# A decoder layer in one kernel: finer waits in the mixer, the merge and the two paired weight blocks

## The reference

```python
xn = rmsnorm(x, g_norm_mix)
proj = xn @ w_in                                  # conv b/c/h, q/k/v, z, a, beta, two merge gates
y_a = (b_c * causal_conv(c_c * h_c)) @ w_out_a    # branch a
o   = gated_delta_chunked(q, k, v, g, beta, s0)
y_b = (normed(o) * silu(z)) @ w_out_dn            # branch b
gate_a, gate_b = jnp.split(jax.nn.sigmoid(gates), 2, axis=-1)
h = x + (gate_a * y_a + gate_b * y_b) @ w_o
h = h + peer(rmsnorm(h, g_norm_ffn), w_query, ...)   # 8 heads, 16 of 16384 experts per token
return rmsnorm(h, g_norm_final)
```

## Time and profile before

| | us |
|---|---|
| median of 3 runs | 3488.58 |
| lowest, highest | 3487.09, 3494.86 |
| span of the profiled execution, first to last instruction | 3500.7 |
| PE busy in it | 3350.9 (96%) |
| DVE busy | 2591.7 (74%) |
| ACT busy | 1018.7 (29%) |
| POOL busy | 977.2 (28%) |

### The profile page before, as it was taken

How to read it: one execution, slowest core, us unless ns; L and a number is a source line. 1 busy time by engine, 2 the same in 40 slices (tenths; PEclk the granted TensorE clock), 3 DMA queues, 4 the chain that set the end, 5 groups by cost and what they waited for, 6 DMA issues and landing times.

```text
span 3500.7 us, 56614 instructions
## 1 busy us (share of the span) xinstructions
PE 3350.9 (96%) x21384; PEld 3291.5 (94%) x21384; DVE 2591.7 (74%) x4995; ACT 1018.7 (29%) x1349; POOL 977.2 (28%) x773
## 2 busy tenths in 40 slices
PE   6999999999998999998998899999999999999996
PEld 6999999899998999998997899999999999999996
DVE  5554444233343379999997899999999999999996
ACT  5742222321322232222543122222222222222222
POOL 0000000000000111111002555555555555555550
PEclk8999999999999999999999999999999999999998
DMA  2111011111322232334889999899998999999992
GB/s 105 40 45 36 29 36 64 68 48 42 141 85 73 89 107 102 106 112 136 266 266 307 333 337 328 318 327 326 338 329 317 327 327 340 328 321 321 329 326 104
DMA packets 304353, 698.46 MB, mean 200 GB/s; under 512 B 23873, under 2 KB 124225, under 8 KB 303201
## 3 DMA queue, kind: packets, MB, share of 16 engines
q0 software_dynamic: 98592, 362.97, 28.5%
q1 hardware_dynamic: 104112, 276.89, 23.3%
q10 hardware_dynamic: 101520, 56.89, 5.3%
HBM read 604.44 MB, written 92.22 MB: 199 GB/s over the span
## 4 chain that ended last, share of the span: by engine, by line
PE 77%; DVE 17%; DMA 2%; DVEq 2%; ACT 1%; issue 1%; ACTq 0%; SPq 0%; PEldq 0%
PE PS L1532 29%; PE PS L365 16%; PE PS L1515 14%; PE PS L1223 6%; PE PS L1253 5%; DVE HOTG L2052 3%; PE PS L1447 3%; PE PS L380 1%; DVE HOT L2048 1%; DVE HOT L2049 1%; DVE fold L1980 1%; DVE besti L1924 1%; DVE sc L1915 1%; DVE besti L1916 1%; DVEq L1978 1%
## 5 line engine op out<-in xcount | busy, mean ns | idle before, releaser
L1532 PE MATMUL PS<-AH,VH 128*128 128x368 f32 x2048 | 513.8, 332 | 20.4 <-DVE VL L2075 10.9
L1532 PE MATMUL PS<-AH,VL 128*128 128x368 f32 x2048 | 515.2, 332 | 0.0
L1532 PE MATMUL PS<-AL,VH 128*128 128x368 f32 x2048 | 509.7, 330 | 0.0
L746 POOL DMA_INDIRECT SLOT<-rows_u,EID x256 | 346.4, 1353 | 578.5 <-DVE XLF L2091 257.5
L746 POOL DMA_INDIRECT SLOT<-rows_v,EID x256 | 333.7, 1304 | 205.7 <-DVE SLOT L2082 167.5
L1532 PEld LDWEIGHTS PS<-AH,VH 128*128 128x128 f32 x2048 | 365.2, 189 | 22.7 <-DVE VL L2075 12.1
L1532 PEld LDWEIGHTS PS<-AL,VH 128*128 128x128 f32 x2048 | 366.2, 189 | 0.0
L1532 PEld LDWEIGHTS PS<-AH,VL 128*128 128x128 f32 x2048 | 365.8, 189 | 0.0
L2091 DVE SCALAR_TENSOR_TENSOR XLF<-SLOT,GA,XLF 128x1024 f32<-128x1024 f32 x256 | 328.0, 1281 | 0.5 <-DMA SLOT<-rows_v,EID 0.2
L1109 ACT ACTIVATE VH<-VRAW 128x512 fp32r<-128x512 f32 x256 | 157.8, 628 | 567.7 <-PE PS L1532 567.7
L2082 DVE SCALAR_TENSOR_TENSOR SLOT<-SLOT,XHF 128x1024 f32<-128x1024 f32 x256 | 312.6, 1221 | 3.3 <-DMA SLOT<-rows_u,EID 3.3
(11 more groups left out here) (331 smaller groups left out, 6478.3 us busy)
## 6 DMA issues: line engine op xcount, KB each, us to landing
RAW<-experts_u SPq DMA_DIRECT2D x128, 512.0 KB, 6.4
VRAW<-experts_v SPq DMA_DIRECT2D x256, 256.0 KB, 5.8
gate_matrices<-stg ACTq DMA_DIRECT2D x21, 2048.0 KB, 10.2
GW<-gate_matrices SPq DMA_DIRECT2D x96, 384.0 KB, 7.2
RAW<-weights SPq DMA_DIRECT2D x69, 512.0 KB, 3.6
activations<-AS SPq DMA_DIRECT2D x64, 368.0 KB, 2.4
AS<-activations SPq DMA_DIRECT2D x64, 368.0 KB, 3.0
GW<-gate_matrices SPq DMA_DIRECT2D x32, 320.0 KB, 6.0
```

The source lines that it names most:

```text
L746: pool.indirect_dma_start(out=SLOT[n % NSLOT][:, :], out_offset=None, in_=table, in_offset=bass.IndirectOffsetOnAxis(ap=ids, axis=0)).then ...
L1532: mm = pe.matmul(PS[:, 4 + 2 * (d % 2) + t, 0:CH], w[:, d % 2, c * P:c * P + P], x[:, c, t * CH:t * CH + CH], start=(c == 0 and n == 0), s ...
```

## The change

It has three parts. (1) `pair_products` takes the two blocks together for the first five chunks only, then the last three chunks of the first block and after them the last three of the second. (2) Ahead of the Y loop PE no longer waits for `bl_done` but for `free_c` (set 1 read), and the BH unit waits chunk by chunk; `free_c` 18 (set 0 read) stands ahead of the OH unit. The two initial counts of `y_read` and of `free_h` are given early. (3) XH and XL of a merged row are made within the Y loop, right after the row's add, by ACT and DVE; the W_o units wait for set 1 and set 0 to be read (`y_read` 17 and 18) and chunk by chunk for `ml_done`, which they did before. 

```diff
--- before.py
+++ after.py
@@ -371,16 +371,19 @@
 
         def pair_products(pe, first, base):
 
-            for k in range(KD):
-                pe.wait_ge(xl_done, base + k + 1)
-                for s in (first, 1 - first):
-                    for n in range(3):
-                        for t in range(3):
-                            w, x = ((WH, XH), (WH, XL), (WL, XH))[n]
-                            mm = pe.matmul(PS[:, 3 * s + t, 0:TH], w[:, s, k * P:k * P + P],
-                                           x[:, k, t * TH:t * TH + TH], start=(k == 0 and n == 0), stop=(k == KD - 1 and n == 2))
-                    if k == KD - 1:
-                        mm.then_inc(unit_done, 1)
+            both = KD - 3
+            order = [(k, s) for k in range(both) for s in (first, 1 - first)]
+            order += [(k, s) for s in (first, 1 - first) for k in range(both, KD)]
+            for k, s in order:
+                if s == first:
+                    pe.wait_ge(xl_done, base + k + 1)
+                for n in range(3):
+                    for t in range(3):
+                        w, x = ((WH, XH), (WH, XL), (WL, XH))[n]
+                        mm = pe.matmul(PS[:, 3 * s + t, 0:TH], w[:, s, k * P:k * P + P],
+                                       x[:, k, t * TH:t * TH + TH], start=(k == 0 and n == 0), stop=(k == KD - 1 and n == 2))
+                if k == KD - 1:
+                    mm.then_inc(unit_done, 1)
 
         rms_sems = {n: {k: sem(f"{n}_{k}") for k in ("sq", "sum", "mm", "ln", "rn")} for n in ("na", "nb", "nc")}
 
@@ -988,11 +991,8 @@
                     row = HID[:, ds(2 * i + q, 1), :].rearrange("p n t -> p (n t)")
                     act.activation(row, row, ACT.Sigmoid).then_inc(sig_done, 1)
                     act.activation(sig[:, q, :], sig[:, q, :], ACT.Sigmoid).then_inc(sig_done, 1)
-
-            act.wait_ge(m_done, KD)
-            act.wait_ge(unit_done, filled(unit_of(B_O - 1)))
-            for k in range(KD):
-                act.activation(XH[:, k, :], HID[:, k, :], ACT.Copy).then_inc(mh_done, 1)
+                    act.wait_ge(m_done, 2 * i + (q + 1))
+                    act.activation(XH[:, ds(2 * i + q, 1), :].rearrange("p n t -> p (n t)"), row, ACT.Copy).then_inc(mh_done, 1)
 
             with act.Fori(0, KD // 2) as i:
                 for r in range(2):
@@ -1383,19 +1383,24 @@
                     products(pe, 1 - r, 1 - r, XH, XL).then_inc(unit_done, 1)
 
             pe.wait_ge(ol_done, H)
-            pe.wait_ge(bl_done, H)
+            pe.wait_ge(free_c, B_Y - B_Z + 1)
             with pe.Fori(0, KD // 2) as i:
                 for q in range(2):
                     pe.wait_ge(lo_done, 2 * i + (B_Y + q + 1))
                     pe.wait_ge(y_read, 4 * i + (2 * q + 1))
-                    products(pe, (1 + q) % 2, 1, BH, BL, range(0, H)).then_inc(unit_done, 1)
+                    products(pe, (1 + q) % 2, 1, BH, BL, range(0, H), ready=(bl_done, 0) if q == 0 else None).then_inc(unit_done, 1)
+                    if q == 0:
+                        pe.wait_ge(free_c, B_Y - B_Z + 2)
                     pe.wait_ge(y_read, 4 * i + (2 * q + 2))
                     products(pe, (1 + q) % 2, 0, OH, OL, range(H, KD), H).then_inc(unit_done, 1)
 
+            pe.wait_ge(y_read, 2 * KD + 1)
             with pe.Fori(0, KD // 2) as i:
                 for r in range(2):
                     pe.wait_ge(lo_done, 2 * i + (B_O + r + 1))
                     pe.wait_ge(free_h, 2 * i + (r + 1))
+                    if r == 1:
+                        pe.wait_ge(y_read, 2 * KD + 2)
                     products(pe, 1 - r, 1 - r, XH, XL, ready=(ml_done, 0) if r == 0 else None).then_inc(unit_done, 1)
             pe.wait_ge(free_h, KD + 2)
             rms_pe(pe, rms_sems["nb"], rn)
@@ -1787,6 +1792,8 @@
                     g_lows(NPAIR, f"d{s}")
             dve.wait_ge(l2_ln, 2 * H + 1 + H)
             dve.drain().then_inc(free_c, 2)
+            dve.drain().then_inc(y_read, 2)
+            dve.drain().then_inc(free_h, 2)
             g_lows(NPAIR, "s")
             for h in range(H):
                 row = QKV[:, h, :]
@@ -1848,7 +1855,6 @@
                 dve.wait_ge(bh_done, i + 1)
                 dve.tensor_tensor(BL[:, i, :], bc[:, :], BH[:, i, :].bitcast(F32), ALU.subtract).then_inc(bl_done, 1)
 
-            dve.drain().then_inc(y_read, 2)
             with dve.Fori(0, KD // 2) as i:
                 for q in range(2):
                     row = thirds(HID[:, ds(2 * i + q, 1), :].rearrange("p n t -> p (n t)"))
@@ -1861,10 +1867,10 @@
                     dve.tensor_tensor(thirds(sig[:, q, :]), pset(0), thirds(sig[:, q, :]), ALU.mult).then_inc(y_read, 1)
                     dve.drain()
                     dve.tensor_tensor(row, row, thirds(sig[:, q, :]), ALU.add).then_inc(m_done, 1)
-            dve.drain().then_inc(free_h, 2)
-            for k in range(KD):
-                dve.wait_ge(mh_done, k + 1)
-                dve.tensor_tensor(XL[:, k, :], HID[:, k, :], XH[:, k, :].bitcast(F32), ALU.subtract).then_inc(ml_done, 1)
+                    dve.wait_ge(mh_done, 2 * i + (q + 1))
+                    dve.tensor_tensor(thirds(XL[:, ds(2 * i + q, 1), :].rearrange("p n t -> p (n t)")), row,
+                                      thirds(XH[:, ds(2 * i + q, 1), :].rearrange("p n t -> p (n t)")).bitcast(F32),
+                                      ALU.subtract).then_inc(ml_done, 1)
 
             rms_zero(dve, rms_sems["nb"], rn)
             with dve.Fori(0, KD // 2) as i:
```

## The result

| | before | changed |
|---|---|---|
| median, us | 3491.72 (4 runs) | 3475.89 (4 runs) |
| lowest, highest | 3487.09, 3495.04 | 3472.35, 3479.23 |
| span of the profiled execution | 3500.7 | 3474.6 |

The ratio is 0.9947, with a 95% interval of 0.9935 to 0.9959: 18.5 us of 3491.7 gained, between 14.3 and 22.7. Forecast were 3468.8 us and a gain of 19.8, within 3463 to 3477.

What follows compares the result with a forecast made beforehand. PE, busy 96% of the span, was taken as the bound, so its waits cost time. Gains of 5.7 + 2.3 + 4.4 + 7.4 = 19.8 us from 3488.6 gave 3468.8 us, range 3463 to 3477.

Steps and rivals of the forecast that it cites:

- Bound: Whole kernel: PE busy 96% of the span, so its waits are kernel time; four single waits make 15.9 us.
- First pair: Unit behind the first pair: gap 4.25 to 1.35 us, full clock behind it; 2.9 + 2.8 = 5.7 us gained.
- rival (b): Unit behind the first pair still starts slow: 17.0 us won, 3471.6 us; chance 0.10.
- Second pair: Behind the second pair: WL no longer late, 2.3 us gained; rows already fast, so no clock to win.
- Entry of the Y loop: First Y units start early, the third waits 2.6 us for the gates' product; 4.4 us gained, not 6.9.
- rival (a): New gap of 2.6 us at the third Y unit takes the clock down: 17.6 us won, 3471.0 us; chance 0.16.
- (a) and (b) together: Clock falls at the third Y unit and the unit behind the first pair starts slow: 3473.8 us; chance 0.04.
- Split in the loop: First W_o unit starts 5.5 us earlier and loses 1.9 us of slow rows: 7.4 us, with 1.4 us to spare.
- Rival (c): Y loop: table loads cost ACT twice their length, two-load halves 1.2 us late, four times; 3473.4 us, chance 0.04.
- Rival (d): Loop entries: another wait still holds PE, parts 2 and 3 give nothing; 8.0 us won, 3480.6 us, chance 0.06.
- Rival (e): Y loop: ring of ACT and DVE turns slower than PE; at 15.5 us 41.6 lost, 3510 us; chance 0.03.
- Behind 1118 us: Everything later hangs on PE or chains starting from it and moves as a block; clock falls worth 2 us either way.

Runs made afterwards that it cites:

- six copies: Changed kernel with six more ACT copies to XH in each Y-loop turn, each with a drain: 3505.49 us, 1.0033 of the kernel before.
- three copies: Changed kernel with three more ACT copies to XH in each Y-loop turn, each with a drain: 3486.22 us, 0.9978 of the kernel before.

## Why the prediction came out as it did

**Bound.** Right for the four entries: in each trace the stretch around an entry that is gone is shorter by it, or by what the next wait leaves of it. It doesn't hold of the whole list: the waits for WL in the expert part (L1447 before), which no part touches, come to 7.7 to 14.6 us over the ten profiles, and the times don't follow them.

**First pair, 5.7 us.** The gap went as written, 1.34 us left for 1.35. The slow rows went too: with the pairs the unit behind is 11.8 us long in all seven profiles that have them, so rival (b) didn't happen. What the forecast had too large is what stood there before. It took 14.56 us from the one profile at hand; the two other kernels without the pairs have 13.17 and 13.95:

```profile
59.57 1.22 PE L365 MATMUL PS<-XH,WH 128*128 128x352 f32 x3 [4.25 <-ACTq L785]
...
72.74 0.38 PE L1199 MATMUL PS<-C,ab 4*128 4x4 f32 x2
```

This is the kernel with the BH and BL waits alone. The same gap of 4.25 us cost 1.3 to 2.7 us of slow rows, and the term is 4.3 to 5.7, not 5.7.

**Second pair, 2.3 us.** With the pairs alone the stretch from the first W_o read to the first row behind the query units is 194.3 us, before 196.7, and with either of the other parts alone 196.7 as well: 2.4. The idle time was right. In the changed kernel WL is there at 1095.73 and PE comes at 1096.46:

```profile
1094.50 1.23 DVE L352 TENSOR_TENSOR WL<-RAW,WH 128x1024 fp32r<-128x1024 f32 x1 [6.51 <-ACT WH L347]
...
1096.46 0.65 PE L365 MATMUL PS<-XH,WH 128*128 128x352 f32 x3
```

But "no clock to win" held in one profile only. Three kernels have this gap of 2.13 us: in before the rows behind it are fast, in the kernels with the waits alone and with the split alone they are slow. The latter:

```profile
1104.38 1.18 PE L365 MATMUL PS<-XH,WH 128*128 128x352 f32 x3 [2.13 <-DVE WL L352]
1105.36 1.08 PE L365 MATMUL PS<-XL,WH 128*128 128x352 f32 x3
```

In the two profiles of the changed kernel the stretch is 3.0 and 3.2 us shorter than before; slow rows at other places of it differ too, so the term is 2.4 to 3.2.

**Entry of the Y loop, 4.4 us.** The step that mattered held: a finer wait gives what the next wait leaves, here the gates. Forecast was a gap of 2.6 us; it is 2.19, since the gates land 0.2 us sooner behind the BL and PE follows DVE after 0.05 us, not 0.15. Then rival (a) came true: the clock fell at this gap in both profiles of the changed kernel and in that of the waits alone (2.19, 2.15, 2.11 us). The two kernels with extra copies have the gap too (2.26, 2.19 us), and there it stayed up. The window's granted clock shows it (columns as in the earlier trace rows):

```profile
880.00:885.00 5.00, 4.74 (x20) 4.74 (x21) 3.57 (x4) 2.16 (x3) 0.94 (x2) 0.66 0.10 14
```

0.66, where 1.00 is 2.4 GHz and 0.50 is 1.2. With it the place is worth 4.6 - 1.7 = 2.9 us in this trace and 2.4 in the kernel with this part alone; rival (a) priced it at 4.4 - 2.2 = 2.2. Its 2.2 us of slow rows came without a working of their own, between the 1.9 and 2.9 taken from other places; the three falls cost 1.65 to 1.67, under both. The term that failed is the 4.4, and what failed in it was the chance of 0.16 (0.20 with the case of (a) and (b) together) for a fall behind a gap this long, where three of five profiles show one. The Trainium skill, "TensorE: Matmul & The Clock Gate", section "Loop structure matters more than you think", says that a long wait for a transfer between every two matmuls makes PE go cold. The waits here are short, 2.1 to 2.3 us, and the clock fell at three of five all the same; with the transfers taken out of the way it stayed up.

**Split in the loop, 7.4 us.** Right in every piece: 74.58 - 69.12 = 5.5 us and 13.88 - 11.95 = 1.9, against 5.5 and 1.9. The middle says 7.6 with this part alone. The runs say 5.9, with an interval that holds 7.4. The cover has 1.25 us left for 1.4 forecast.

**Rival (c)**, table loads at twice their length, would have made gaps in every second turn; none is there, and the activation starts 0.02 us behind its load (876.43 + 1.28, then 877.73). The drain of 1.38 us that the Trainium skill gives beside each load in "ScalarE: Activation LUTs", section "What ACT_TABLE_LOAD costs", isn't seen in this loop, neither ahead of a load (896.46 + 1.08 = 897.54, then 897.56) nor behind one. **Rival (d)** is refuted by the entry that is gone, in the kernel with that part alone.

**Rival (e)'s price** was too high: 41.6 us for a ring of 15.5, counted as 4.0 of waiting and 1.2 of slow rows in each of eight turns. With six copies the turns are (16.8 + 14.3) / 2 = 15.6 us and the loss 29.0. It is paid in seven turns, not eight, since the first row's product stands ahead of all copies. And where the ring sets the pace a turn lasts as long as the ring, and slow rows lie inside PE's next wait: the turns from 911.23 and from 942.37 both last 14.3 us, the first at full pace with 2.54 us of wait at its end, the second with slow rows and 0.96. Only where PE is the bound again, as with three copies, do slow rows add.

**The sum and the level.** By the traces the terms are 4.3 to 5.7, 2.4 to 3.2, 2.4 to 2.9 and 7.4 to 7.6: 16.5 to 19.4 us in place of 19.8, and the runs say 18.5. That is 1.3 us of the 7.1. Another 2.7 are the distance between the ratio's 18.5 and the 15.8 by which the two medians of four runs differ, and 3.1 are the level: the forecast put the gain under the median of the first three runs, 3488.58; with one run more it was 3491.72. Over 29 and 17 runs on two chips it was 3494.87 and 3495.63. The changed kernel repeats within 0.6 us (3475.89, 3476.52). With a level 3 to 7 us too low the time still came within the range, by 1.1 us; that is in part luck. The 12.1 us between span and median of before, which the forecast took as given, seem to be no property of the profiler: in the later kernels each run's own time is 1.7 us above its span (3476.33 and 3474.6). By that rule the profiled execution of before took some 3502.4 us, longer than any other run of it on record (at most 3502.18). The difference of the two spans, 26.1 us, would have told 7.6 too much. Where it comes from is seen in code that the change doesn't touch. Granted clock of 500 to 600 us, before, changed, and changed once more (columns as in the earlier trace rows, the clock is the third number from the end):

```profile
500.00:600.00 100.00, 96.91 (x696) 94.85 (x695) 44.13 (x84) 23.37 (x50) 0.00 (x0) 0.93 0.10 33
```

```profile
500.00:600.00 100.00, 95.73 (x730) 93.35 (x729) 47.37 (x96) 23.38 (x50) 1.07 (x2) 1.00 0.14 44
```

```profile
500.00:600.00 100.00, 97.32 (x702) 95.23 (x701) 42.42 (x79) 23.38 (x50) 1.07 (x2) 0.93 0.11 38
```

One program has 1.00 here once and 0.93 the next time, and gets 730 or 702 matmuls done in the 100 us. Between the first row sums of the q/k/v stage (some 80 us in, L1191 before) and the start of the middle, which no part touches, before took 790.0 us and the nine others 783.1 to 788.5. **Behind 1118 us** the forecast took everything to move as a block. The code from the query units to the last norm took 2285.5 us before and 2281.1 and 2280.9 in the two profiles of the changed kernel, but 2279.1 to 2283.9 in the three kernels with one part each; before is the longest of the ten profiles, but the change can't be told from that spread.

## What to carry to other kernels

A wait made finer is worth the distance to the next thing that is late, so look up when every other input of the unit arrives before counting the old gap as won: here it was two gates' transfers, issued behind an event the change didn't move, and fetching them early was worth 4.1 us more by the trace, where the finer wait itself had given 2.4 to 2.9. Work moved into a loop was free here while its ring of engines was shorter than the turn of PE, the bound; count the ring by its rows, with the handovers, and load it on purpose once to see where it breaks (1.25 us by the trace, 3.4 us put in, 2.1 us late). Take the gain from the gaps, and the level from many runs: the median of three was 6 to 7 us off, and two profiles of different luck differ by more than most edits are worth.

## What the hardware showed that I hadn't expected

**The length of a gap doesn't decide whether the clock falls**, among the gaps seen here of 2.1 to 3.5 us. With three copies, 2.10 us took it down at 905.67 and at 932.63 and not at 959.61, in one loop, with the same rows before and behind; with six copies it fell behind 2.57, 2.54 and 3.44 and not behind 3.46. Behind the second pair's gap of 2.13 us it stayed up in before and fell in two other kernels; in before it stayed up behind 3.19 too. At one and the same place, the third Y unit, it fell behind 2.19, 2.15 and 2.11 us and not behind 2.26 and 2.19. What does decide isn't settled by these runs. The gap of 1.34 us behind the first pair never took it down, in six profiles.

**The clock was low around small matmuls too.** PE is without an idle moment in the transposes of a and beta (4 x 4 tiles, 3.9 to 4.9 us of them, from 68.13 in the changed kernel), and yet within them or behind them the clock is at 0.50 in all ten profiles, for a time that differs between two executions of one program. No run takes the transposes away, so that they are the cause is not shown. Changed, and changed once more:

```profile
72.00:74.00 2.00, 2.00 (x10) 1.98 (x9) 1.84 (x3) 0.00 (x0) 0.00 (x0) 0.50 0.00 0
...
76.00:78.00 2.00, 2.00 (x15) 2.00 (x14) 0.00 (x0) 1.97 (x5) 0.00 (x0) 1.00 0.00 0
```

```profile
72.00:74.00 2.00, 2.00 (x9) 1.99 (x8) 1.85 (x2) 0.00 (x0) 0.00 (x0) 0.50 0.00 0
...
76.00:78.00 2.00, 2.00 (x8) 2.00 (x8) 0.00 (x0) 1.97 (x4) 0.00 (x0) 0.50 0.00 0
```

The unit behind them starts at 72.06 and 72.02 and the next stage at 79.41 and 80.68: 1.3 us of difference between two executions of one program, with the same work and no gap of PE in it. No edit of this study tried to mend it.
